# One decoder layer on one core: the expert table in two halves, and two gathers for each slot

## What is computed

```
s1 = einsum('bshd,kd->bshk', q[..., 0, :], key1)          # 128 keys a side, 8 heads
s2 = einsum('bshd,kd->bshk', q[..., 1, :], key2)
v1, i1 = lax.top_k(s1, 16);  v2, i2 = lax.top_k(s2, 16)
cand = (v1[..., :, None] + v2[..., None, :]).reshape(B, S, 8, 256)
sc, ci = lax.top_k(cand, 16)
expert = e1 * 128 + e2                                    # one of 16384
gate = softmax(sc)
ue = u[expert];  ve = v[expert]                           # rows of 1024 floats each
hid = gelu(einsum('td,ted->te', xt, ue))
out = einsum('te,ted->td', gate * hid, ve)
```

## Time and profile before

| | |
|---|---|
| median of 2 runs | 1170.58 us (1163.55 and 1177.61) |
| the profiled execution | 1177.78 us, its span 1176.0 us |
| first gather of the mixer / last one begins | 500.72 us / 1153.60 us |
| gathers | 256, each 1 MB |
| mean share of the DMA engines from 600 to 1160 us | 1.01, 418 GB/s |

### The profile page before, as it was taken

The page is one execution under the profiler, slowest core; times in us unless marked ns, Lnnn a source line. Parts: engine busy times, 40 slices in busy tenths (PEclk is TensorE's granted clock), DMA queues, the critical chain, the costliest instruction groups (busy, mean ns, idle before and its releaser), DMA issues.

```text
span 1176.0 us, 16361 instructions
## 1 busy us (share of the span) xinstructions
PE 965.0 (82%) x5708; PEld 599.0 (51%) x5708; DVE 703.9 (60%) x1810; ACT 233.6 (20%) x587; POOL 291.3 (25%) x293
## 2 busy tenths in 40 slices
PE   6999999999999999988887667766676776667766
PEld 5888888978878878765442222222222222222222
DVE  0362332096325241545877887788688778877885
ACT  2006124214312010221211110211111011102111
POOL 0000000030003000033335433443343444334431
PEclk8997999999999999999998889988979898899899
DMA  7342332222212243497999999999999999999996
GB/s 278 108 146 105 110 141 97 96 86 82 73 37 73 73 171 140 179 359 303 375 398 395 422 422 422 422 422 421 422 372 423 422 421 422 422 421 422 421 422 259
DMA packets 46402, 329.34 MB, mean 280 GB/s; under 512 B 5264, under 2 KB 5648, under 8 KB 6800
## 3 DMA queue, kind: packets, MB, share of 16 engines
q0 software_dynamic: 36864, 268.45, 55.4%
q1 hardware_dynamic: 8928, 58.48, 13.7%
q10 hardware_dynamic: 560, 1.70, 0.4%
HBM read 327.57 MB, written 1.05 MB: 279 GB/s over the span
## 4 chain that ended last, share of the span: by engine, by line
PE 52%; DMA 17%; DVE 16%; issue 10%; ACT 3%; POOL 1%; another core or an unknown queue 1%; DVEq 0%; POOLq 0%; ACTq 0%
PE psum_proj L612 21%; DMA pool_mem<-in_experts,pool_mem 16%; PE psum_job L994 8%; PE psum_proj L625 5%; PE psum_proj L994 3%; PE psum_proj L961 3%; DVE pool_mem L1755 3%; PE psum_job L844 2%; DVE pool_mem L521 2%; DVE pool_mem L1696 2%; DVE pool_mem L1693 1%; DVE pool_mem L1733 1%; DVE pool_mem L1700 1%; PE psum_job L632 1%; PE psum_job L647 1%
## 5 line engine op out<-in xcount | busy, mean ns | idle before, releaser
L994 PE MATMUL psum_job<-pool_mem 64*64 64x512 f32 x1536 | 351.9, 676 | 91.9 <-DVE pool_mem L521 87.9
L1826 POOL DMA_INDIRECT pool_mem<-in_experts,pool_mem x256 | 267.4, 1044 | 505.9 <-PE psum_job L994 232.8
L1755 DVE CUSTOM_DVE_ANT_0 pool_mem<-pool_mem 128x1024 f32<-128x1024 f32 x256 | 312.8, 1222 | 107.4 <-DMA pool_mem<-in_experts,pool_mem 101.2
L612 PE MATMUL psum_proj<-pool_mem 128*128 128x256 f32 x1152 | 267.1, 392 | 11.6 <-DVE pool_mem L1315 9.1
L994 PEld LDWEIGHTS psum_job<-pool_mem 64*64 64x64 f32 x1536 | 113.4, 149 | 288.9 <-issue 287.7
L612 PEld LDWEIGHTS psum_proj<-pool_mem 128*128 128x128 f32 x1152 | 224.5, 197 | 49.4 <-DVE pool_mem L1315 9.1
L994 PE MATMUL psum_proj<-pool_mem 64*64 64x512 f32 x512 | 144.5, 688 | 85.1 <-DVE pool_mem L521 83.4
L1253 ACT ACTIVATE pool_mem<-pool_mem 128x1 f32<-128x1 f32 x256 | 51.1, 202 | 486.0 <-DVE pool_mem L1755 441.4
L994 PEld LDWEIGHTS psum_proj<-pool_mem 64*64 64x64 f32 x512 | 40.0, 149 | 171.2 <-issue 170.3
L1808 POOL TENSOR_TENSOR pool_mem<-pool_mem,const 128x256 f32<-128x256 f32 x24 | 18.5, 793 | 357.7 <-DVE pool_mem L1559 298.5
L521 DVE TENSOR_SCALAR pool_mem<-const,pool_mem 128x64 f32<-128x64 f32 x256 | 79.9, 312 | 34.6 <-ACT pool_mem L1253 32.6
(11 more groups left out here) (252 smaller groups left out, 782.0 us busy)
## 6 DMA issues: line engine op xcount, KB each, us to landing
pool_mem<-in_weights SPq DMA_DIRECT2D x51, 1024.0 KB, 4.8
pool_mem<-in_experts,pool_mem POOLq DMA_INDIRECT x256
pool_mem<-in_xT SPq DMA_DIRECT2D x1, 1024.0 KB, 4.9
pool_mem<-in_memT SPq DMA_DIRECT2D x1, 1024.0 KB, 10.7
pool_mem<-in_x ACTq DMA_DIRECT2D x1, 1024.0 KB, 7.6
out<-pool_mem SPq DMA_DIRECT2D x2, 512.0 KB, 5.5
const<-in_const SPq DMA_DIRECT2D x1, 552.5 KB, 13.5
rows<-in_rows SPq DMA_DIRECT2D x1, 512.0 KB, 15.8
```

The lines of the kernel that those rows point to most:

```text
L612: ins = mm(o[:, m, :], lhsT=w[:, k, m * P:(m + 1) * P], rhs=src[:, k, :], start=(k == 0), stop=(k == KT - 1))
L994: ins = mm(sum_bank(t, odd, d)[strip:strip + 64, :], lhsT=diag[rows_, g % DIAGS, :], rhs=slot[g % SLOTS][rows_, D + 512 * d:D + 512 * d + ...
L1755: ins = V.tensor_tensor_reduce(u, u, xn_tok[:, t, :], 1.0, 0.0, ALU.mult, ALU.add, hid[:, par, s_:s_ + 1])
L1826: G_.indirect_dma_start(slot[s_ % SLOTS], None, t_in["experts"], bass.IndirectOffsetOnAxis(ap=expert_i[:, par, s_:s_ + 1], axis=0)).then_i ...
```

## The change

The table is passed as two: `in_experts_lo` holds rows 0 to 8191 and `in_experts_hi` rows 16383 down to 8192, in reverse. Beside the expert's number `e` a second number `16383 - e` is kept (`expert_j`). Each slot is filled by two gathers of 128 places each, one from each table, with a bounds check against 8191 and with `oob_is_err=False`: a place above the bound is passed over. Exactly one of the two numbers of a place is within the bound. The second gather of a slot (`high`) first waits until the first one has landed, and it is issued `LAG = 3` steps after it. The dot waits for 32 on `slot_in` in place of 16. DVE has two more instructions for each head in `choose_experts`.

```diff
+EXPERTS = KEYS * KEYS
+LAG = 3
...
+                s(V.tensor_scalar(expert_r[:, :], expert_f[:, :], -1.0, float(EXPERTS - 1), ALU.mult, ALU.add)); w()
                 V.tensor_copy(expert_i[:, par, :], expert_f[:, :]).then_inc(sg["experts_ok"], 1)
+                V.tensor_copy(expert_j[:, par, :], expert_r[:, :]).then_inc(sg["experts_ok"], 1)
...
-                    dve.wait_ge(slot_in[s_ % SLOTS], uses * 16 + 16)
+                    dve.wait_ge(slot_in[s_ % SLOTS], uses * 32 + 32)
...
+            def gather(table, places, par, s_):
+
+                G_.indirect_dma_start(slot[s_ % SLOTS], None, t_in[table],
+                                      bass.IndirectOffsetOnAxis(ap=places[:, par, s_:s_ + 1], axis=0),
+                                      bounds_check=EXPERTS // 2 - 1, oob_is_err=False).then_inc(slot_in[s_ % SLOTS], 16)
+
+            def high(i, par, s_):
+
+                wait_alone(pool, slot_in[s_ % SLOTS], i * 128 + (64 * par + 32 * (s_ // SLOTS) + 16))
+                gather("experts_hi", expert_j, par, s_)
+
...
-                    pool.wait_ge(sg["experts_ok"], i * 2 + (par + 1))
+                    pool.wait_ge(sg["experts_ok"], i * 4 + (2 * par + 2))
                     for s_ in range(TOPK):
                         if s_ % GROUP == 0:
 
                             wait_alone(pool, sg["group_free"], i * (2 * HEAD_GROUPS) + (HEAD_GROUPS * par + s_ // GROUP + 1))
-                        G_.indirect_dma_start(slot[s_ % SLOTS], None, t_in["experts"],
-                                              bass.IndirectOffsetOnAxis(ap=expert_i[:, par, s_:s_ + 1], axis=0)
-                                              ).then_inc(slot_in[s_ % SLOTS], 16)
+                        gather("experts_lo", expert_i, par, s_)
+                        if s_ >= LAG:
+                            high(i, par, s_ - LAG)
+                    for s_ in range(TOPK - LAG, TOPK):
+                        high(i, par, s_)
...
-        "experts": np.concatenate([a["peer_u"][0], a["peer_v"][0]], axis=1),
+        "experts_lo": experts[:EXPERTS // 2], "experts_hi": experts[:EXPERTS // 2 - 1:-1],
```

More of the change, by code:

```diff
@@ L357, in build @@
         expert_f = tail(F32, TOPK)
+        expert_r = tail(F32, TOPK)
         expert_i = tail(U32, 2, TOPK)
+        expert_j = tail(U32, 2, TOPK)
         gate_e = tail(F32, 2, TOPK)
@@ L1815, in _ @@
                                              ALU.add).then_inc(sg["xt0"], 1)
-            pool.wait_ge(sg["experts_ok"], 1)
+            def gather(table, places, par, s_):
[5 more added lines that the diff above has]
+                gather("experts_hi", expert_j, par, s_)
+            pool.wait_ge(sg["experts_ok"], 2)
             pool.sem_inc(sg["group_free"], RING_GROUPS)
@@ L1866 @@
         two(a["att_q_gain"][0]), two(a["att_k_gain"][0]), _vec(a["mem_q_gain"]), _vec(a["mem_k_gain"]), _vec(a["ffn_norm_gain"])], axis=1)
+    experts = np.concatenate([a["peer_u"][0], a["peer_v"][0]], axis=1)
     arrays = {
```

## The result

| | before | changed |
|---|---|---|
| median of the runs | 1170.58 us | 1432.27 us (1429.14 and 1435.39) |
| profiled execution, span | 1177.78, 1176.0 us | 1435.39, 1433.6 us |
| ratio | | 1.223, interval 1.208 to 1.238 |
| a head (first gather's start to last one's, by 16) | 40.8 us | 57.3 us |

The direction was forecast, and that the slots and POOL take over from the data; the size was not: 1285 us, with a range that ended at 1400. The loss is 262 us where 107 had been summed up.

What follows compares the result with a forecast made beforehand. Data bound the kernel before; with the change, reuse of eight slots, POOL just under it. Sixteen heads of 47.7 us (45.2 plus 2.5 of stalls), 763.6 us, with start and tail gave 1284 us; forecast 1285, range 1225 to 1400.

Steps and rivals of the forecast that it cites:

- What bounds the kernel before, and what the change spends: Mixer stage: data at 422 GB/s bound it; the change spends POOL's spare issue rate and the queue of eight whole slots.
- the ring of eight slots: Reuse of a slot after eight steps: claimed as the new bound, 2.83 us a step, 45.2 us a head.
- Two gathers are slower than the data: POOL issuing both gathers of a slot: 2.69 us against 2.48 us for the slot's data.
- End of a head: Last second gathers of a head: a 1.0 us wait for slot 15's first landing, counted within the 45.2 us.
- two stalls: POOL waiting before the first gathers of slots 8 and 12 while DVE chooses experts: 2.1 and 0.4 us a head.
- POOL just under the ring: Steps of the mixer: POOL's 2.69 us a step lies just below the 2.83 us set by slot reuse.
- 3T + p: Time from a slot's first gather to its second: three steps T of 2.83 us plus one gather's POOL time p, 1.34 us.
- Price of a gather on POOL: POOL's time for each of 512 gathers: 1.34 us, from today's mean of 1.044 plus a gap of 0.30.
- Landing of a half: From a half gather's start to its dot: 5.6 us, or 4.8 without unevenness between DMA engines.
- From a dot to a free slot: Dot, diagonal, matmuls (1.95 us) and the 0.80 us until POOL starts: 4.36 us in all.
- Rival 4: Places not passed over: each gather moves all 128 rows, 537 MB, about 1810 us; chance 4 in 100.
- rival 1: Slow passing over: testing each place makes POOL's descriptor work longer than about 1.35 us; 1400 to 1690 us; 9 in 100.

## Why the prediction was off, step by step

**What bounds the kernel before, and what the change spends:** right. The bytes written stayed, POOL's spare rate went, and the ring of eight slots and POOL took over from the data. "Two gathers are slower than the data" is the 120 us that stay without any lag or wait; that the number of slots and the lag count is borne out by LAG = 2 and 4.

**End of a head: taken as part of the ring's time, the step that failed most.** The sum spreads a head over 16 even steps of 2.83 us and adds two stalls. By the three stretches that is 22.6 + 2.1 = 24.7 us, 11.3 + 0.4 = 11.7 and 11.3; measured are 24.9, 13.9 and 18.7. So 7.4 of the 9.8 us that a head is too long, nearly 120 of the 151 us that the profiled execution lies above the sum, stand between step 12's first gather and the next head's. POOL has 11 gathers of its own there (four first ones, seven second ones), where the stretch before has 8: 11 x 1.48 = 16.3 us, and before the last of them it waits for slot 15's first to land, 1.9 us in the mean (0.3 to 2.9). The order on POOL was known: with the prediction's own 1.34 and its 1.0 us of wait this is 15.7 us and not 11.3. "POOL just under the ring" compares two means over a head; in the first stretch the slots bind, in the last POOL. This is counted from rows, since no run moved these gathers. But with u and v as two tables the last stretch takes 17.3 us with the landing wait and 16.2 without it, which is 11 of POOL's own times.

That the first stretch agrees is partly luck. Step 0's second gather goes out 7.4 us after its first, not 3T + p = 9.8, because four first gathers follow each other at a head's start; this makes good what the landings and the matmuls took longer (7.4 + 6.6 + 4.9 + 6.2 = 25.1 us in the head shown, against 9.8 + 5.6 + 4.9 + 4.4).

**Price of a gather on POOL: 1.34 us, mis-sized.** It was 1.18 + 0.30 = 1.48. Of the difference 0.05 is the bounds check; the rest is that more gathers begin inside a dot and stand still for what is left of it. The rows of up to 2.0 us in the earlier trace rows were in front of me, and I took them into a mean as if it did not depend on how often a gather starts beside a dot.

**Landing of a half: 5.6 us, mis-sized.** The landings on the chain from 600 to 1400 us have a median of 6.5 us in the changed kernel (5.2 to 9.0), and of 6.0 to 6.1 where halves are even, here two pieces of the kernel with nothing passed over:

```profile
758.05 6.26 DMA pool_mem<-in_experts_lo,pool_mem
...
772.87 6.23 DMA pool_mem<-in_experts_hi,pool_mem
```

The fastest landing in that kernel is 4.1 us, so the 4.8 for an even half can be had; the likeliest reason for the rest, argued and not tested, is that at one half of 1.24 us of data each 1.3 to 1.5 us each lands behind another. The unevenness makes some 0.5 us of landing instead of 0.8, but 45 us of time instead of 27. With 6.6 and 1.48 the ring's time is (6.6 + 1.48 + 4.36)/4 = 3.11 us, 49.8 us a head instead of 45.2, or 24.9, 12.4 and 12.4 by stretches. So these two prices move the sum by 73 us, but they alone would leave 6.3 us a head in the last stretch and 1.5 in the middle one.

**From a dot to a free slot: 4.36 us, mis-sized.** It had 1.95 us of matmuls where the chain shows 3.7 before steps 8 and 12, behind 12.1 and 4.9 us in which PE stood still. In the head shown that is the middle stretch's excess: its turn of the ring took 13.5 us, with matmuls 1.7 us longer than in the equation and a landing 0.8 us shorter than 6.6. The run with half of the matmuls puts the whole term at about 35 us; there the first stretch falls to 23.0 us and the last to 18.0, while the middle one stays at 14.0, so what binds the middle in the mean stays open.

**The extra reads:** not forecast. Rival 4 had the right fact in part (rows are read for places that are passed over, as the HBM row and the packets show) with the wrong price.

**The range** took in a slow check and even halves, but held the landing at no more than 5.6 us. The measured time lies in the range of rival 1, but not by its mechanism: a gather's row has a mean of 1.18 us, under the 1.35 that rival 1 asks for. The shares of DMA (0.86) and GB/s (293) show that to hold it there was not safe: the engines are busy for 86% of the time with what should fill 70%.

## What to carry to other kernels

A stage that is bound by its data is fed by two reserves, the issuer's spare rate and the depth of what is queued; before splitting a transfer, work out 2 x issue time against the transfer's time, and the number of slots against the time for which one is held, since at the edge one more step of lag cost first 27 us and then 173. Write a queue's order down for a whole round, seams included, and count what it has to issue between one wait and the next: a mean over the round hides a stretch in which the issuer alone is too slow. Take a landing from transfers that follow each other at the new rate, not from one on an empty queue.

## What the runs showed of the hardware

- An indirect gather's place beyond the bound is not written, but with 8 KB rows it has its packet (73728 against 36864), and a row is read for it from HBM: 596 against 328 MB. With 8 KB rows or 256-byte rows the time was the same (1396 and 1394 us).
- The bounds check costs 0.05 us of POOL for 128 places (0.990 against 0.937 us).
- A gather that begins while DVE runs a dot with both operands in SBUF takes up to 1.07 us longer (2.05 against 0.98), until just before the dot's end; with one of them in PSUM it does not (1.18 to 1.00 us in the mean).
- After PE had stood still for 12 us its matmuls took 3.7 us a step at a granted clock of 0.50, against 1.9 at 1.00. After 4.9 us it was 3.7 us as well, at 0.62 to 0.70 in the two stretches of 5 us around it.
